# Scores of a forgetting attention in two fp32r matmuls from split operands, and 21 convolution taps issued later

## What is computed

```
h = rmsnorm(x, g_mix); proj = h @ w_in            # a_in, q, k, v, f_logit, gate_a, gate_b
a = a_in[:, :512] * sigmoid(a_in[:, 512:])
a = causal_depthwise_conv(a, w_dw, 31 taps) + b_dw
y_conv = silu(layernorm(a)) @ w_conv_out
q, k = rmsnorm per head of 64, times g_q, g_k     # 8 heads
c = cumsum(log_sigmoid(f_logit + b_forget))       # per head and token
s[q, k] = (q . k) / 8 + c[q] - c[k]               # for k <= q, else -inf
y_attn = (softmax(s) @ v) @ w_attn_out
x = x + (sigmoid(gate_a) * y_conv + sigmoid(gate_b) * y_attn) @ w_out
x = x + (silu(h2 @ w1) * (h2 @ w2)) @ w_ffn_out   # h2 = rmsnorm(x)
```

## Time and profile before

| | us |
|---|---|
| median of 3 runs | 2735.84 |
| lowest, highest | 2734.06, 2737.50 |
| the profiled execution's span | 2734.5 |
| TensorE busy | 2631.4 (96%) |
| VectorE busy | 1831.5 (67%) |
| ScalarE busy | 1273.0 (47%) |
| POOL busy | 482.7 (18%) |

### The profile page before, as it was taken

How to read it: one execution, slowest core, us unless ns; L and a number is a source line. 1 busy time by engine, 2 the same in 40 slices (tenths; PEclk the granted TensorE clock), 3 DMA queues, 4 the chain that set the end, 5 groups by cost and what they waited for, 6 DMA issues and landing times. The chain is left out here.

```text
span 2734.5 us, 35669 instructions
## 1 busy us (share of the span) xinstructions
PE 2631.4 (96%) x13421; PEld 2203.5 (81%) x13421; DVE 1831.5 (67%) x2255; ACT 1273.0 (47%) x1918; POOL 482.7 (18%) x665
## 2 busy tenths in 40 slices
PE   8999999999999999999999999989998599999996
PEld 7788888888898877777888898878877588888885
DVE  4377776742437888885556433389845788888887
ACT  4244443331235333333435312178833377777775
POOL 6711110000003222222011320012232300000102
PEclk9999999999999999999999999999999799999998
DMA  8700010121323455556764532001234699999998
GB/s 308 252 24 13 13 36 16 47 62 47 116 85 102 133 159 166 182 192 248 233 200 149 146 72 69 13 20 25 77 132 166 235 379 393 396 395 393 396 395 272
DMA packets 249513, 461.88 MB, mean 169 GB/s; under 512 B 16588, under 2 KB 138176, under 8 KB 247936
## 3 DMA queue, kind: packets, MB, share of 16 engines
q1 hardware_dynamic: 218944, 352.73, 36.8%
q0 software_dynamic: 30288, 106.84, 11.9%
q10 hardware_dynamic: 112, 0.03, 0.0%
HBM read 384.79 MB, written 65.32 MB: 165 GB/s over the span
## 5 line engine op out<-in xcount | busy, mean ns | idle before, releaser
L503 PE MATMUL ps<-r,r 128*128 128x512 f32 (+2 forms) x10316 | 2267.4, 378 | 9.7 <-DVE r L667 3.8
L503 PEld LDWEIGHTS ps<-r,r 128*128 128x128 f32 x10316 | 1845.4, 188 | 358.8 <-issue 11.0
L480 ACT ACTIVATE r<-f 128x2048 fp32r<-128x2048 f32 (+2 forms) x339 | 504.2, 1494 | 389.1 <-PE ps L503 383.7
L3693 DVE TENSOR_TENSOR r<-f,r 128x2048 fp32r<-128x2048 f32 x188 | 429.1, 2291 | 63.8 <-ACT r L480 62.7
L488 DVE TENSOR_TENSOR r<-f,r 128x1024 fp32r<-128x1024 f32 (+1 forms) x151 | 169.2, 1134 | 315.7 <-ACT r L480 315.6
L503 PE MATMUL ps<-f,f 128*128 128x64 f32 (+3 forms) x1410 | 218.4, 304 | 0.3 <-DVE f L3641 0.3
L503 PEld LDWEIGHTS ps<-f,f 128*128 128x128 f32 (+1 forms) x1410 | 179.6, 192 | 22.9 <-issue 19.3
L871 DVE SCALAR_TENSOR_TENSOR f<-f,misc,f 128x1023 f32<-128x1023 f32 (+29 forms) x120 | 148.1, 1260 | 0.0
L1972 ACT ACTIVATE r<-f 128x512 fp32r<-128x512 f32 x140 | 87.3, 629 | 73.0 <-PE ps L503 58.1
L1161 ACT ACTIVATE f<-ps,misc 128x128 f32<-128x128 f32 (+7 forms) x64 | 47.5, 742 | 144.3 <-DVE misc L1150 144.3
L1979 DVE TENSOR_TENSOR r<-f,r 128x512 fp32r<-128x512 f32 x140 | 108.2, 776 | 6.8 <-ACT r L1972 6.7
(11 more groups left out here) (343 smaller groups left out, 2178.2 us busy)
## 6 DMA issues: line engine op xcount, KB each, us to landing
f<-in_w_gate_dram SPq DMA_DIRECT2D x64, 1024.0 KB, 8.2
f<-in_w_up_dram SPq DMA_DIRECT2D x64, 1024.0 KB, 9.9
f<-in_w_down_dram SPq DMA_DIRECT2D x64, 1024.0 KB, 8.0
f<-in_w_in_dram SPq DMA_DIRECT2D x56, 512.0 KB, 4.2
f<-in_w_ada_dram SPq DMA_DIRECT2D x96, 256.0 KB, 4.8
f<-in_w_ffn_in_dram SPq DMA_DIRECT2D x80, 256.0 KB, 4.1
hid_scratch<-f POOLq DMA_DIRECT2D x77, 256.0 KB, 2.8
f<-hid_scratch SPq DMA_DIRECT2D x35, 512.0 KB, 5.2
```

Of the source, the lines that this page charges most:

```text
L480: self.act.activation(hi, raw, ACT.Copy).then_inc(self.sem(st.name + "_hi"), 1)
L503: return self.pe.matmul(o, left, right, start=start, stop=stop, skip_group_check=True)
L3693: self.dve.tensor_tensor(es.lo[i % 4], es.raw[i % 8], es.hi[i % 4].bitcast(F32), ALU.subtract).then_inc(self.sem("e_lo"), 1)
```

## The change

It replaces each fp32 matmul of the scores (66 rows deep) by two fp32r matmuls. The first has 128 rows: the rounded k stands twice (`KA`), under it the rounded q above and the rest of q below (`QA`). The second has 68 rows: the rest of k (`KB`) by the rounded q (`QB`), and four rows for c, now split in two parts for q and two for k. The product of the two rests is left out. For this:

- ACT makes three copies of a turned tile in place of two, POOL copies rounded q and k to partitions 64 to 127 (`pool_copy_qk`), DVE computes the rests (`dve_low_qk`). The scores and the next projection wait for them (`qk_lo`, `qk_dup`).
- DVE has two more small operations on c, and the buffers of squares and of v are one and ten in place of two and sixteen tiles.
- `TAPS` has 20 taps in 16 steps in place of 26, and the two blocks of 4 taps in the gate stage become 12.

```
-    TAPS = (3, 3, 2, 3, 1, 1, 1, 1, 1, 1, 1, 1, 2, 3, 1, 1)
+    TAPS = (2, 2, 2, 2, 1, 1, 1, 1, 1, 1, 1, 1, 1, 1, 1, 1)
...
     def dve_attention(self):
...
                 self.dve_mean_squares(tg, t)
+            lg, lt = self.tile(s, 3)
+            if lg is not None and (lt or not lg):
+                self.dve_low_qk(lg, lt)
             g, u = self.unit(s, 0)
             if g is not None:
                 self.dve_largest(g, u)
+            if lg and lt == 0:
+                self.dve_low_qk(lg, lt)
...
     def pe_project(self, g, t, quarter):
...
             pe.wait_ge(*sem("qk_ev", 8 * g + t - 1))
+            pe.wait_ge(*sem("qk_lo", 8 * g + t - 1))
...
     def pool_project(self):
...
-            heads = lambda x: x[:, t, 2 * g:2 * g + 2].rearrange("p (h o) -> p h o", o=1)
-            pool.tensor_copy(self.QK[j][:, 0:2, 65:66], heads(self.cc))
-            pool.tensor_copy(self.QK[j][:, 2:4, 64:65], heads(self.ncc)).then_inc(sem("pj_aug"), 1)
+            heads = lambda x: x[:, 8 * t + 2 * g:8 * t + 2 * g + 2, :].bitcast(F32)
+            pool.tensor_copy(self.QK[j][:, 0:2, 64:66], heads(self.cc))
+            pool.tensor_copy(self.QK[j][:, 2:4, 66:68], heads(self.ncc)).then_inc(sem("pj_aug"), 1)
+            self.pool_copy_qk(g, t)
...
     def act_turn_qk(self, g, t):
...
+        act.activation(self.QB[t % 2][0:68], self.heads_of(slice(0, 68), t)[:, 0:2, :], ACT.Copy,
+                       scale=self.gqk[0:68, 0:1])
         if g:
             act.wait_ge(*sem("at_qk", 16 * g))
-        act.activation(self.QT[0:66, :, sl], v[:, 0:2, :], ACT.Copy, scale=self.gqk[0:66, 0:1])
-        act.activation(self.KT[0:66, :, sl], v[:, 2:4, :], ACT.Copy, scale=self.gqk[0:66, 1:2]).then_inc(
+        act.activation(self.KA[r0, :, sl], self.heads_of(r0, t)[:, 2:4, :], ACT.Copy,
+                       scale=self.gqk[r0, 1:2])
+        act.activation(self.KB[64:68, :, sl], self.heads_of(slice(64, 68), t)[:, 2:4, :], ACT.Copy).then_inc(
             sem("qk_ev"), 1)
+
+    def pool_copy_qk(self, g, t):
+        pool, sem, n = self.pool, self.sem, 8 * g + t
+        sl, r0, r1 = slice(t * P, (t + 1) * P), slice(0, 64), slice(64, 128)
+        pool.wait_ge(*sem("qk_ev", n + 1))
+        pool.tensor_copy(self.QA[t % 2][r0], self.QB[t % 2][r0].bitcast(F32))
+        pool.tensor_copy(self.KA[r1, :, sl], self.KA[r0, :, sl].bitcast(F32)).then_inc(sem("qk_dup"), 1)
+        pool.wait_ge(*sem("qk_dup", n + 1))
+
+    def dve_low_qk(self, g, t):
+        dve, sem, n = self.dve, self.sem, 8 * g + t
+        sl, r0, r1 = slice(t * P, (t + 1) * P), slice(0, 64), slice(64, 128)
+        dve.wait_ge(*sem("qk_ev", n + 1))
+        dve.scalar_tensor_tensor(out=self.QA[t % 2][r1], in0=self.heads_of(r0, t)[:, 0:2, :], scalar=self.gqk[r0, 0:1],
+                                 in1=self.QB[t % 2][r0].bitcast(F32), op0=ALU.mult, op1=ALU.subtract)
+        dve.scalar_tensor_tensor(out=self.KB[r0, :, sl], in0=self.heads_of(r0, t)[:, 2:4, :], scalar=self.gqk[r0, 1:2],
+                                 in1=self.KA[r0, :, sl].bitcast(F32), op0=ALU.mult, op1=ALU.subtract).then_inc(
+            sem("qk_lo"), 1)
...
     def pe_scores(self, g, u):
...
         pe.wait_ge(*sem("qk_ev", 8 * g + i + 1))
+        pe.wait_ge(*sem("qk_lo", 8 * g + i + 1))
+        pe.wait_ge(*sem("qk_dup", 8 * g + i + 1))
...
-            m = self.mm(o, self.QT[0:66, h, i * P:(i + 1) * P], self.KT[0:66, h, c0:c0 + w], True, not diag)
+            self.mm(o, self.QA[i % 2][:, h, :], self.KA[:, h, c0:c0 + w], True, False)
+            m = self.mm(o, self.QB[i % 2][0:68, h, :], self.KB[0:68, h, c0:c0 + w], False, not diag)
...
     def dve_gate_a(self):
...
             self.low(self.ws, self.i_ga + mt + 3)
-            self.dve_taps(4 if mt < 2 else 124)
+            self.dve_taps(12 if mt < 2 else 124)
```

More of the change, by code:

```diff
@@ L190, in memory @@
         self.zf, self.zb, self.lf = m(64), m(64), m(64)
-        self.Lp, self.cc, self.ncc = m(8, 8), m(8, 8), m(8, 8)
+        self.Lp = m(8, 8)
+        c0 = self.mpos - 256
+        parts = nc.alloc_sbuf_tensor_at("cparts", [P, 264], F32R, offset=base + 201 * 1024 + c0 // 8 * 32)[:, c0 % 8:]
+        self.cc, self.ncc = [parts[:, 128 * j:128 * j + 128].rearrange("p (a b) -> p a b", b=2) for j in range(2)]
         self.rows_a, self.rows_b, self.crow = f(104, P), f(104.5, P), f(105, P)
@@ L201, in memory @@
         self.fgT = f(105, 1024)
-        self.QT, self.KT, self.VV = f(64, 2, 1024), f(72, 2, 1024), [f(80, 8, P), f(165, 8, P)]
-        self.QK = [f(84 + 1.03125 * j, 4, 66) for j in range(2)]
-        self.SQ = [f(86.0625 + j, 256) for j in range(2)]
-        self.OM = [f(88.0625, P), m(P)]
+        self.KA, self.KB = self.r(64, 2, 1024), self.r(72, 2, 1024)
+        self.QA, self.QB = [self.r(80 + j, 2, P) for j in range(2)], [self.r(82 + j, 2, P) for j in range(2)]
+        self.VV = [f(165 + 0.5 * j, P) for j in range(8)] + [f(87.125 + 0.5 * j, P) for j in range(2)]
+        self.QK = [f(84 + 1.0625 * j, 4, 68) for j in range(2)]
+        self.SQ = f(86.125, 256)
+        self.OM = [f(88.125, P), m(P)]
         self.PB = [f(89 + 4 * j, 1024) for j in range(2)]
@@ L893, in dve_cumulate @@
         dve.wait_ge(*sem("cum_mm", 1))
-        dve.tensor_copy(self.cc.rearrange("p a b -> p (a b)"), self.ps[:, 6, 0:64]).then_inc(sem("cc"), 1)
-        dve.tensor_scalar(self.ncc.rearrange("p a b -> p (a b)"), self.ps[:, 6, 0:64], -1.0, None,
-                          ALU.mult).then_inc(sem("cc"), 1)
+        c = self.ps[:, 6, 0:64]
+        part = lambda x, k: x[:, :, k]
+        dve.tensor_copy(part(self.cc, 0), c).then_inc(sem("cc"), 1)
+        dve.tensor_scalar(part(self.ncc, 0), c, -1.0, None, ALU.mult).then_inc(sem("cc"), 1)
+        dve.wait_ge(*sem("cc", 2))
+        dve.tensor_tensor(part(self.cc, 1), c, part(self.cc, 0).bitcast(F32), ALU.subtract).then_inc(sem("cc"), 1)
+        dve.scalar_tensor_tensor(out=part(self.ncc, 1), in0=c, scalar=-1.0, in1=part(self.ncc, 0).bitcast(F32),
+                                 op0=ALU.mult, op1=ALU.subtract).then_inc(sem("cc"), 1)
     UNITS = [(i, h) for i in range(NT) for h in range(2)]
@@ L1047, in act_squares @@
         pq, pk, _ = self.segments(g, t)
-        n, j = 8 * g + t, t % 2
+        n = 8 * g + t
         act.wait_ge(*sem("pj_mm", n + 1))
-        if n >= 2:
-            act.wait_ge(*sem("pj_st", n - 1))
-        act.activation(self.SQ[j][:, 0:P], pq, ACT.Square)
-        act.activation(self.SQ[j][:, P:2 * P], pk, ACT.Square).then_inc(sem("pj_sq"), 1)
+        if n:
+            act.wait_ge(*sem("pj_st", n))
+        act.activation(self.SQ[:, 0:P], pq, ACT.Square)
+        act.activation(self.SQ[:, P:2 * P], pk, ACT.Square).then_inc(sem("pj_sq"), 1)
     def act_values(self, g, t):
         self.act.wait_ge(*self.sem("pj_nrm", 8 * g + t + 1))
-        if g >= 2:
-            self.act.wait_ge(*self.sem("at_pv", 16 * (g - 1)))
-        self.act.copy(self.VV[g % 2][:, t, :], self.segments(g, t)[2]).then_inc(self.sem("pj_v"), 1)
+        n = 8 * g + t
+        if n >= 10:
+            self.act.wait_ge(*self.sem("at_pv", 16 * ((n - 10) // 8 + 1)))
+        self.act.copy(self.VV[n % 10], self.segments(g, t)[2]).then_inc(self.sem("pj_v"), 1)
     def dve_mean_squares(self, g, t):
@@ L1115, in act_turn_qk @@
[L1115 to L1116 removed]
+        act, sem, n = self.act, self.sem, 8 * g + t
+        sl, r0 = slice(t * P, (t + 1) * P), slice(0, 64)
+        act.wait_ge(*sem("qk_T", n + 1))
+        if n >= 2:
+            act.wait_ge(*sem("at_qk", 2 * n - 2))
+        act.activation(self.QB[t % 2][0:68], self.heads_of(slice(0, 68), t)[:, 0:2, :], ACT.Copy,
+                       scale=self.gqk[0:68, 0:1])
         if g:
             act.wait_ge(*sem("at_qk", 16 * g))
[L1119 removed]
```

25 lines of the change are left out of this document (12 added, 13 removed).

## The result

The changed kernel takes 2757.59 us (median of 4 runs, 2752.87 to 2760.58) against 2736.23 us for the kernel before in runs on the same chip: a ratio of 1.0081, 95% interval 1.0069 to 1.0092. That is 21.4 us slower, where 3.5 were forecast, and outside the range of 2732 to 2750. The profiled execution has a span of 2751.6 us, 17.1 more than before's.

What follows compares the result with a forecast made beforehand. The prediction took TensorE to bound the attention stage, with no slack in the gate stage. Attention -23, moved taps +24.1 and clock +2.4 gave +3.5 us: 2738.0 span, 2739.5 forecast; own range 2735 to 2744, wider range 2732 to 2750.

Steps and rivals of the forecast that it cites:

- The gate stage: Gate stage on VectorE: first split to last addition grows from 23.3 us with 13 taps to 47.8 with 34.
- So it comes there 24.1 us too early: TensorE ahead of the `ln_sum` matmuls: it stands still 24.1 us for the moved taps, part of it ahead of tile 6.
- The clock: TensorE behind the gate-stage stall: a low granted clock costs 2.4 us, between 1.7 and 3.3.
- The scores: Attention stage on TensorE: two fp32r matmuls per block in place of fp32 save 28.9 us of its queue.
- Waits of 6 us in the attention stage: Attention stage: net 2 us of the saving lost at each of three group changes, so it shortens by 23 us.
- TensorE sets the pace there, with an ACT/DVE chain close behind at the group changes: Attention stage: TensorE's records cover 325.7 of 336 us, VectorE's 240.1; its only large wait is 6.7 us for ACT's copy.
- it is worst at the group changes: Attention stage, late row maximum: 1.3 us given away in step 31, 0.6 in step 32; 0.2 to 0.3 late from i = 4.
- The taps taken from steps 13, 16, 17 and 19 give back some 0.5 us.: Attention stage, group changes: removing these taps returns some 0.5 us of the time lost to waits.
- DVE's load stays as it was: Attention stage on VectorE: 22 us of added rests (0.35 us each) against 24.5 us of taps that leave.
- POOL and ACT: Attention stage, each of 32 tiles: two POOL copies at 0.6 us each and one more ACT copy at 0.46 us.
- The second: Rival: the split chain becomes the bound in the attention stage, price 10 us more, +13.7, 2749.5 us; chance 0.17.
- The sign to watch for: Attention stage: forecast wrong if TensorE's waits for ACT's copy, the rests or POOL's copies together exceed 17 us.

Runs made afterwards that it cites:

- e5_rests_behind: Split scores with the old tap numbers and one tap ahead of the copy L1242, plus the rests moved behind the row maximum in all steps: 2724.40 us, ratio 0.9970.
- e11_short_rests: Changed kernel with taps on 8 tokens only, plus rests cut to 8 of 128 columns from the second head group: 2706.02 us, attention stage 291.7 us.

## Why the prediction was wrong, point by point

- **The gate stage: right.** 47.8 us from the first split to the last addition were forecast, 47.9 measured. "So it comes there 24.1 us too early": +24.3. Of it 3.5 and 17.4 us are waiting, and 3.1 are the 48 matmuls between the two waits, 14.07 us where 48 x 0.228 = 10.9 are usual. 3 to 4 us ahead of tile 6 were forecast.
- **The clock: right.** 2.4 forecast, 2.7 measured.
- **The scores: nearly right.** At 1024 keys from start of scores to values 285.74 to 286.73, 0.99 us, 0.97 forecast. Over all 64 units this time falls by 26.8 us, 28.9 forecast. Scores over 128 keys take 0.28 us as before, where 0.1 each had been put down as saved.
- **Waits of 6 us in the attention stage: wrong, and this step decided.** Some 20 us of the saving became waiting, so the stage gave 5.6 and not 23. Two sentences of it fail. "TensorE sets the pace there, with an ACT/DVE chain close behind at the group changes": the chain was close behind in wide steps too, 6.50 us beside 6.62 of matmuls in step 34, and it closes on itself through the taps. Looking at the row of the waits (6.7 us in all), I took a small wait for slack. It says only that the chain was not yet the longer one; how near it is stands in the starts of its links, which the trace of before had: from steps 31, 33 and 35 the chain already set the distance of the maxima. And "it is worst at the group changes": step 31 did give 1.7 us away (1.3 forecast) and step 32 0.7 (0.6 forecast), but steps 33 and 34, for which I had 0.2 to 0.3 at most, gave 1.5 and 0.9.
- **"The taps taken from steps 13, 16, 17 and 19 give back some 0.5 us."** Right in size for the wide steps 33 and 34 (nothing: 1.56 and 1.48 with the old taps, 1.57 and 1.49 with the new), for the reason that I had not seen: the ones taken were the ones ahead of the copy. In the whole stage they gave 5.7, most of it where a step went from 2 taps to 1 behind the copy, as step 30 (1.26 to 0.24).
- **"DVE's load stays as it was": right and beside the point.** VectorE is busy 226.9 us where it was 221.3, of 303. A rest takes 0.48 us and not 0.35, 8 us more in the stage; not its load but its place in the loop matters, as one tap moved past the copy in each wide step shows with 16 us at equal load.
- **POOL and ACT: forecast too dear.** POOL's copies take 0.39 each, 0.6 forecast; ACT's third 0.375, 0.46 forecast. The groups of the changed kernel (busy us, mean ns, idle before and who ended it):

```profile
L1161 DVE SCALAR_TENSOR_TENSOR r<-ps,misc,r 64x256 fp32r<-64x256 f32 x32 | 15.3, 478 | 24.6 <-ACT r L1146 23.9
...
L1154 POOL CAST r<-r 64x256 fp32r<-64x256 f32 x32 | 12.5, 392 | 1.4
L1146 ACT ACTIVATE r<-ps 4x256 fp32r<-4x256 f32 x32 | 12.0, 375 | 0.4
```

- **The rivals.** The second was nearest in sign and place (the chain becomes the bound in the attention stage) and had a price of 10 us; it was 17.4 (23 less 5.6). Its mechanism is there, but isn't what decided: the rests lengthen the loop by up to 1.0 us into odd wide steps (30 to 31 and 32 to 33), and in steps 31 and 33 `e5_rests_behind` takes 0.9 and 1.0 us of wait away; over the stage they carry 1.3 us by `e5_rests_behind` and 3.2 by `e11_short_rests`, while one tap a step behind the copy carries 16. These are not shares of one sum: either the tap or the rests out of the loop empties most of step 33's wait. The sign to watch for that the prediction named, more than 17 us of waits for ACT's copy, did come, and for the reason that the maximum was late.
- **What the median has beyond the terms.** -6.2 + 24.3 + 2.7 = 20.8, and the medians differ by 21.4. The error, 17.9 us, is the attention stage's (17.4); some 2 of it are the scores' size, the rest the waits.

## What to carry to other kernels

When the bounding engine is to be made faster, follow the chain that feeds it once round through all the queues, from one operation to the same one of the next step, and compare its length with the engine's own work in a step: here 6.50 beside 6.62 us, and a saving of 0.8 went into waiting. Filler work on an in-order engine is priced by where it stands and not by how much of it there is: ahead of an operation that waits anyway it was free here, behind it and ahead of the next link of the chain it cost nearly its duration (1.1 to 1.2 of 1.2 us), and when some of it is taken away, look which of the two is left. Work that is moved to the stage behind, where neither engine had slack, cost its whole duration.
